# Up projections of two squared-ReLU feed-forwards: eight block products against seven

## What is computed

```
h    = rms_norm(x, g)                      # x: 512 tokens x 1024
u    = relu(h @ w1)                        # w1: 1024 x 4096
x    = x + (u * u) @ w2                    # w2: 4096 x 1024
```

## Time and profile before

| | |
|---|---|
| three runs | 2274.29, 2274.32, 2277.49 us; median 2274.32 |
| profiled execution: span from first to last instruction | 2272.1 us |
| its own time around the span | not given apart; the median of the runs is 2.2 us over the span |
| TensorE busy | 2247.1 us, 99% |
| VectorE / ScalarE / GpSimd busy | 1230.8 / 777.3 / 168.5 us |
| granted TensorE clock | tenths of 9 (90% and more) in all 40 slices |

### The profile page before, as it was taken

How to read it: one execution, slowest core, us unless ns; L and a number is a source line. 1 busy time by engine, 2 the same in 40 slices (tenths; PEclk the granted TensorE clock), 3 DMA queues, 4 the chain that set the end, 5 groups by cost and what they waited for, 6 DMA issues and landing times.

```text
span 2272.1 us, 28489 instructions
## 1 busy us (share of the span) xinstructions
PE 2247.1 (99%) x11659; PEld 1825.8 (80%) x11659; DVE 1230.8 (54%) x1464; ACT 777.3 (34%) x1024; POOL 168.5 (7%) x135
## 2 busy tenths in 40 slices
PE   9999999999999999999999999999999999999999
PEld 7888888878888888887876788888877868888888
DVE  6434446597543355575567644344468864544443
ACT  4222234244422323353247322222334573212221
POOL 2000001030100100020011100000101201000000
PEclk9999999999999999999999999999999999999999
DMA  5223223310323232232320232232233102323322
GB/s 188 93 93 106 97 79 99 93 61 20 102 92 105 82 109 93 75 110 93 104 65 20 78 107 93 93 100 87 87 106 89 61 20 65 102 93 95 108 86 81
DMA packets 193332, 200.56 MB, mean 88 GB/s; under 512 B 6370, under 2 KB 187378, under 8 KB 193236
## 3 DMA queue, kind: packets, MB, share of 16 engines
q1 hardware_dynamic: 193236, 199.22, 27.7%
HBM read 191.93 MB, written 2.10 MB: 85 GB/s over the span
## 4 chain that ended last, share of the span: by engine, by line
PE 93%; DVE 5%; ACT 1%; issue 1%; DMA 0%; SPq 0%; DVEq 0%; ACTq 0%
PE psum L684 92%; DVE sm L2477 1%; DVE rstd L1976 0%; DVE w_lo L296 0%; PE psum L1165 0%; PE psum L1173 0%; DVE free_x L1958 0%; ACT free_h L1449 0%; DVE free_h L1961 0%; DVE free_x L2599 0%; DVE sm L2597 0%; DVE sm L2303 0%; PE psum L916 0%; DVE xg_lo L1958 0%; DMA gains<-in_gains 0%
## 5 line engine op out<-in xcount | busy, mean ns | idle before, releaser
L684 PE MATMUL psum<-xg_lo,w_hi 128*128 128x512 f32 (+1 forms) x1576 | 608.4, 389 | 0.4 <-ACT free_x L1449 0.4
L684 PE MATMUL psum<-xg_hi,w_hi 128*128 128x512 f32 (+1 forms) x1528 | 596.0, 390 | 4.3 <-DVE xg_lo L1958 1.7
L684 PE MATMUL psum<-xg_hi,w_lo 128*128 128x512 f32 (+1 forms) x1528 | 592.9, 388 | 0.0
L288 ACT ACTIVATE w_hi<-w_raw 128x2048 fp32r<-128x2048 f32 (+1 forms) x178 | 338.7, 1903 | 478.0 <-PE psum L684 478.0
L296 DVE TENSOR_TENSOR w_lo<-w_raw,w_hi 128x2048 fp32r<-128x2048 f32 (+1 forms) x176 | 403.5, 2293 | 162.2 <-ACT w_hi L288 159.0
L684 PE MATMUL psum<-h_hi,w_hi 128*128 128x512 f32 x1144 | 451.7, 395 | 0.3 <-DVE h_lo L1958 0.3
L684 PE MATMUL psum<-h_hi,w_lo 128*128 128x512 f32 x1144 | 445.6, 389 | 0.0
L684 PE MATMUL psum<-h_lo,w_hi 128*128 128x512 f32 x1144 | 445.6, 389 | 0.0
L684 PEld LDWEIGHTS psum<-xg_lo,w_hi 128*128 128x128 f32 x1576 | 295.6, 188 | 62.2 <-ACT free_x L1449 1.4
L684 PEld LDWEIGHTS psum<-xg_hi,w_hi 128*128 128x128 f32 x1528 | 286.9, 188 | 68.9 <-issue 4.6
L684 PEld LDWEIGHTS psum<-xg_hi,w_lo 128*128 128x128 f32 x1528 | 286.9, 188 | 59.1
(11 more groups left out here) (309 smaller groups left out, 2106.8 us busy)
## 6 DMA issues: line engine op xcount, KB each, us to landing
w_raw<-in_mlp_w SPq DMA_DIRECT2D x64, 1024.0 KB, 5.4
w_raw<-in_ffn_w_gate SPq DMA_DIRECT2D x21, 1024.0 KB, 5.3
w_raw<-in_ffn_w_up SPq DMA_DIRECT2D x21, 1024.0 KB, 5.3
w_raw<-in_ffn_w_down SPq DMA_DIRECT2D x16, 1024.0 KB, 5.2
w_raw<-in_diff_w_in SPq DMA_DIRECT2D x12, 1024.0 KB, 5.1
w_raw<-in_w_in SPq DMA_DIRECT2D x9, 1024.0 KB, 5.2
w_raw<-in_dsa_w_in SPq DMA_DIRECT2D x9, 1024.0 KB, 5.1
w_raw<-in_ffn_w_down SPq DMA_DIRECT2D x8, 768.0 KB, 4.5
```

The costliest lines, as they stand in the source:

```text
L288: e.activation(w_hi[:, c % 2, 0:n], w_raw[:, c % 2, 0:n], ACT.Copy).then_inc(sem("hi_done"), 1)
L684: return pe.matmul(out, lhsT, rhs, start=start, stop=stop)
```

## The change

In both feed-forwards, two up blocks at a time (512 hidden features) are computed as a 2x2 block product with seven products in place of eight. The contraction tiles are halved by parity (even and odd k), the 512 tokens in two halves of 256, the hidden features in the two blocks. A product is then 4 k by 2 m by 3 = 24 matmuls of 256 columns.

- **Weights.** A block's load becomes two quarter loads of 512 KB (`fast_loads`). Seven operands a pair ("strips" of 1024 elements a partition) are split high and low: three are raw quarters, four are sums of quarters made by GpSimd (`w_sums`) in the arena. `w_hi` and `w_lo` are used as four strip slots, each free again when its product is done.
- **x.** In `wout2` and `wout3` ScalarE writes the scaled tiles to a buffer, VectorE makes three sums for each pair of tiles (four instructions of 256 columns), then come the split of the plain tiles (1024 elements) and of the sums (768 elements): `fin_sums`, `x_sums`.
- **Results.** ScalarE copies four intermediate results a pair out of PSUM, VectorE adds two of them to other banks, GpSimd adds two. VectorE then applies max(.,0) and `rstd`, and ScalarE squares and makes the high part.
- **Order.** GpSimd's weight sums of the first pair stand between its sums of squares. The loops of these feed-forwards are written out. Several semaphores elsewhere are merged (the constants' loads, the gate, the seed steps); what waits on them waits on the sum.

The core of the diff:

```diff
+        def strip_lo(e, c0, n):
...
+            e.tensor_tensor(lo_, strip_source(pair, i)[0], hi_.bitcast(F32),
+                            ALU.subtract).then_inc(strip_mark("lo", pair, i)[0], 1)
...
+            def fin_sums(p, i):
+                for m in range(2):
+                    a(x_raw(i)[:, m, :], x_res[:, 2 * i + m, :], ACT.Copy,
+                      scale=ngain(p, 2 * i + m)).then_inc(sem("x_scaled"), 1)
+                for t in (2 * i, 2 * i + 1):
...
+                    a(sq[:, t % 2, :], x_res[:, t, :], ACT.Square).then_inc(sem("sq_done"), 1)
+                act.wait_ge(sem("x_sums"), 4 * n + 2)
+                a(xg(p)[0][:, 2 * i:2 * i + 2, :], x_raw(i)[:], ACT.Copy).then_inc(sem("xg_hi_done"), 1)
+                act.wait_ge(sem("x_sums"), 4 * n + 4)
+                a(sx_hi[:, :, i, :], x_sum(i), ACT.Copy).then_inc(sem("xg_hi_done"), 1)
...
+            def x_sums(p, i):
+                tt(z[:, 0, :], e2, o2, ALU.add).then_inc(sem("x_sums"), 1)
+                tt(e2, e1, e2, ALU.subtract).then_inc(sem("x_sums"), 1)
+                dve.wait_ge(sem("x_sums"), 4 * n + 1)
+                tt(z[:, 1, :], z[:, 0, :], e1, ALU.subtract).then_inc(sem("x_sums"), 1)
+                dve.wait_ge(sem("x_sums"), 4 * n + 3)
+                tt(z[:, 2, :], o1, z[:, 1, :], ALU.subtract).then_inc(sem("x_sums"), 1)
...
@@ residual (VectorE)
+                if p_next in FAST.values():
+                    x_sums(p_next, i)
+                    if i < 3 and not split_first:
+                        lo(dve, c + 2 + i)
+                    fin_sums(p_next, i)
+                    if i == 3:
+                        lo(dve, c + 2 + i)
+                    return
...
@@ TensorE, one pair
+                    product(0, range(4))
+                    product(1, range(4))
+                    pe.wait_ge(sem("p_copied"), 4 * pair + 1)
+                    product(2, range(4))
...
+                    pe.wait_ge(sem("p_copied"), 4 * pair + 4)
+                    product(6, range(4))
...
@@ ScalarE, one pair
+                    if q:
+                        split(7 * q + 3)
+                        square(q - 1, 1)
+                    copy(pair, 0, chain, buf_c[:, 0, :])
+                    split(7 * q + 4)
+                    copy(pair, 1, second, buf_c[:, 1, :])
+                    split(7 * q + 5)
+                    copy(pair, 2, chain, buf_d[:, 0, :])
...
+                    split(7 * q + 6)
+                    split(7 * q + 7)
+                    copy(pair, 3, chain, buf_d[:, 1, :])
+                    if q == len(made) - 1:
+                        hi(act, after)
+                    split(7 * q + 8)
+                    split(7 * q + 9)
+                    square(q, 0)
...
@@ GpSimd
+                    if t == 3:
+                        w_sums(pair, (0, 1))
+                    if t == 5:
+                        w_sums(pair, (2, 3))
...
+                        if q + 1 < len(made):
+                            w_sums(pair + 1, (0, 1, 2))
+                        pool.wait_ge(sem("p_copied"), 4 * pair + 4)
...
+                        pool.tensor_tensor(buf_a[:, :, TS:S], by_halves(buf_d[:, 1, :]), by_halves(buf_c[:, 1, :]),
+                                           ALU.add).then_inc(sem("half_p"), 1)
+                        if q + 1 < len(made):
+                            w_sums(pair + 1, (3,))
+                    if g + 1 < len(GROUPS2):
+                        w_sums(made[-1] + 1, range(4))
```

More of the change, by code:

```diff
@@ L125, in gain_columns @@
     return np.ascontiguousarray(g.T)
+FAST = {"mlp0": 5, "mlp1": 7}
 def plan():
@@ new lines, in pairs_of, with wside, raw, strip @@
+        def pairs_of(c0):
+            first = fast_groups[c0]
+            return [i for i in range(first, len(pair_block)) if pair_block[i] - c0 in (2 * (i - first),)
+                    and (i == first or pair_block[i] not in fast_groups)]
+        def wside(c):
+            return (c + turned[c]) % 2
+        def raw(c, half):
+            return w_raw[:, c % 2, half * Q:(half + 1) * Q]
+        def strip(c0, n):
+            s_ = (2 * wside(c0) + n) % 4
+            cols = slice((s_ % 2) * Q, (s_ % 2 + 1) * Q)
+            return w_hi[:, s_ // 2, cols], w_lo[:, s_ // 2, cols]
@@ L283, in hi @@
                 return
+            for c0 in (c, c - 1):
+                if isinstance(j, int) and c0 in fast_groups:
+                    for n in range(2):
+                        strip_hi(e, c0, 2 * (c - c0) + n)
+                    return
             e.wait_ge(sem(f"landed{c % 2}"), 16 * j + 16 * (c // 2 + 1))
@@ L536, in ffn @@
                     else:
[L537 to L540, removed]
+                        fast_loads(c, rows(wu, 0, KT)[:, :, P * f0:P * (f0 + tiles)])
                     c = at[name, g, "down"]
@@ L764, in ffn @@
                     waits = {0: [(sem("h_done"), h0 + tiles // 2 - 1)], tiles - 2: [(sem("h_done"), h0 + tiles // 2)]}
+                    if name in FAST:
+                        waits = {k: [(sem("h_done"), h0 + max(2, k // 2 + 1))] for k in (0, 4, 6)}
                     c = at[name, g, "down"]
@@ new lines, in fast_up, with split, copy, square @@
+            def fast_up(c0, p, entry, h0):
+                made = pairs_of(c0)
+                after = c0 + 2 * len(made)
+                def split(n):
+                    if n < 7 * len(made):
+                        strip_hi(act, c0, n)
+                def copy(pair, j, src, dst):
+                    act.wait_ge(*strip_mark("pe", pair, (0, 1, 2, 4)[j]))
+                    if pair:
+                        act.wait_ge(*((sem("half_c"), pair) if j == 0 else (sem("half_p"), pair) if j in (1, 3) else
+                                      (sem("evac"), pair_block[pair - 1] + 1)))
+                    a(dst, src, ACT.Copy).then_inc(sem("p_copied"), 1)
+                def square(q, s_):
+                    v, n = (buf_a, buf_b)[s_], h0 + 2 * q + s_
+                    act.wait_ge(sem("hmul"), n + 1)
+                    a(v[:], v[:], ACT.Square).then_inc(sem("h_sq"), 1)
+                    act.wait_ge(sem("h_sq"), 2 * (fast_groups[c0] + q) + s_ + 1)
+                    a(hidden(p)[0][:, 4 * q + 2 * s_:4 * q + 2 * s_ + 2, :], v[:], ACT.Copy).then_inc(sem("h_hi_done"), 1)
+                for q, pair in enumerate(made):
+                    chain, second, third = pair_banks(c0, q)
+                    if q:
[6 more added lines that the diff above has]
+                    copy(pair, 2, chain, buf_d[:, 0, :])
+                    if entry and q == 0:
+                        stats(p)
+                    split(7 * q + 6)
[6 more added lines that the diff above has]
+                    square(q, 0)
+                square(len(made) - 1, 1)
+                hi(act, after + 1)
@@ L2730, in _, with add_squares @@
         def _(pool):
-            def add_squares(ready, done, r0, d0, dst):
+            def add_squares(ready, done, r0, d0, dst, between=None):
                 for t in range(1, KT):
@@ L2831, in _ @@
             sua_rounded()
-            fin(5)
+            fast_fin(5)
+            fast_up("mlp0")
             fin(6)
```

372 lines of the change are left out of this document (299 added, 73 removed).

## The result

The changed kernel takes 2311.39 us (median of 4 runs, 2308.94 to 2311.99) where the kernel before takes 2275.18 beside it (4 runs): ratio 1.0154, 95% interval 1.014 to 1.0169. It is slower by 36 us. The profiled execution is the one of 2311.99 us; its span is 2310.2 us.

What follows compares the result with a forecast made beforehand. It took TensorE's number and pitch of matmuls as the bound. Terms -25.6 + 17.7 + 20.6 + 14.8 + 4.2 = +31.7 on a span of 2272.1 gave 2303.8, so a median of 2306 us, range 2255 to 2320.

Steps and rivals of the forecast that it cites:

- Part 1: TensorE's up blocks: 168 matmuls of 256 columns replace 96 of 512, gaining 1.60 us a pair, -25.6 us for 16 pairs.
- The -38: Alternative estimate of the matmul gain in the up blocks, from isolated-matmul times of 109 and 216 ns: some 38 us.
- Part 2: VectorE and GpSimd, both reading two SBUF operands, take turns; GpSimd holds 2.27 us and VectorE 1.08 for 1024 elements.
- Rival A: Entries and groups: GpSimd's turns don't fall on the path, so the kernel is faster, 2258.8 us; chance 0.24.
- Part 3: Feed-forward entries: TensorE waits for the longer VectorE and ScalarE chain plus GpSimd's turns, 17.7 us in `mlp1`, 20.6 in `mlp0`.
- part 5: Clock after the last long wait of each entry: matmuls run at a lower level, +4.2 us in all, bounds 0 and 12.
- Part 4: Groups: TensorE waits before product 2 for ScalarE's copy of product 0, 1.5 us a group, 14.8 for both feed-forwards.
- Rival C: Groups: the down block's low part is late after a further GpSimd turn in each of 8, 2332 us; chance 0.08.
- Squares on ScalarE: Groups: moving the squares from VectorE to ScalarE was claimed to save VectorE nothing on the path.

Runs made afterwards that it cites:

- experiment 11: Changed kernel with first groups at eight products, copy of product 0 first, VectorE making second pairs' weight sums, whole computation done: 2256.43 us, 0.9909 of the kernel before.
- Experiment 1: Changed kernel with GpSimd writing one column of each weight sum in place of 1024, and a 2048-column fill before each entry: 2269.91 us, 0.9969 of the kernel before.
- Experiment 7: Changed kernel with unread 512-column matmuls put where TensorE would wait, at both entries and before product 2 of each second pair: 2307.58 us, 1.0142 of the kernel before.
- experiment 3: Changed kernel with ScalarE copying product 0 before strip 3 and the previous pair's square in each second pair: 2296.98 us, 1.0095 of the kernel before.
- experiment 8: Changed kernel with VectorE making the squares in place of ScalarE: 2336.87 us, 1.027 of the kernel before.
- experiment 6: Changed kernel with GpSimd copying the first operand of each weight sum in place of subtracting the second from it: 2277.90 us, 1.0015 of the kernel before.

## Why the prediction was right

Forecast 2306, measured 2311.4, on the side and by the mechanism forecast. That the number is so near is partly luck: several terms are off by 3 to 8 us and partly offset each other. Step by step:

- **Part 1, -25.6.** Right in kind, a little small. Without waits two pairs take 39.99 us [experiment 11], pitch 0.119, which makes -28.2 for 16 pairs. The -38 by the Trainium skill, "TensorE: Matmul & The Clock Gate", section "Back-to-back issue gap", was further off, as the rows had said. The seven starts a pair cost nothing.
- **Part 2, the turns.** Right: VectorE's instructions end 1.1 us after GpSimd's, and GpSimd's 3.39 us at 1414.40 end 2.27 after VectorE's split (1413.22 + 2.31). Experiment 1 prices them: 41.5 us come back. Rival A (turns off the path) fell with it, and its 2258.8 was too low even without the sums: 2269.9, because the entries alone keep 16 us of waits and slow spells of 7, where I had 10.1.
- **Part 3, the entries, 38.3.** Measured 31.4 of waits, 7 less than forecast, and 11.0 of slow spells, 7 more than part 5 had. Together 42.4 against 38.3 + 4.2 = 42.5: the sum is right because the two errors cancel, which is luck. Experiment 7 suggests that the chain of VectorE sets the whole of it, since the entries lose as much with fewer slow spells; then this part is 4 too small and part 5's term does not lie here. The longest wait was forecast at 7.5 and is 7.2 in `mlp0` and 5.8 in `mlp1`, for tiles 6 and 7, ended by VectorE as said; block 3, the first strip and tiles 4 and 5 were waited for too, as said. The quarter loads landed after 4.5 us (4.9 in the first entry), not 3.6, which the text had priced at 3 us; no run tests whether they are what is missing. The written sum is also 0.2 too high (54.0 - 37.0 + 0.5 is 17.5, not 17.7).
- **Part 4, a group, 14.8.** The place and the chain are right (ScalarE's copy behind square and high part, experiment 3). The size is not: 1.8 to 2.3 us in place of 1.5 (2.6 in the first), 17.9 in all, and the slow spells behind three of these waits, which the step had at nothing, 5.2. Both together are 8 us over the step. **This is the term that was mis-sized**; the 2.6 us by which part 1 was too small offset a third of it. The chain had one square and one high part ahead of the copy, 4.0 us from VectorE's lateness on. In the trace ScalarE has two of each and a strip, and from the end of VectorE's `buf_a` (1418.88) to the end of the copy (1424.53) it is 5.6 us. VectorE's own lateness was put too high in return: `buf_a` ends 2.2 us after product 6 (its last matmul is at 1416.38 + 0.28), not 3.1. So the copy is done 7.9 us after product 6 in place of 7.2.
- **Part 5, the clock, +4.2 net.** Experiment 7 gives 3.8 us for what it took away of the low clock, about the forecast, but by luck: the seat is wrong. I had it behind the last long wait of each entry. Behind those it hides in VectorE's lateness, and it is paid in the groups, after waits of 2.0 to 2.3 us, to which I had given no low clock. The last of the earlier trace rows could have told me: there the granted clock is 0.53 from 2.3 us after TensorE's last matmul on.
- **Rival C** (2332) had the right neighbour: experiment 8 adds work to VectorE in a first pair, and the groups' waits grow, a down block becomes late, and the time is 2337.
- **Squares on ScalarE "save VectorE nothing on the path"** was wrong: they save 25.5 us against VectorE squaring within this scheme. The sentence compared with the kernel before, where VectorE had room.

What stays open: why a slow spell follows some waits of 2.0 to 2.3 us and not others (three of eight in the kernel after, all eight with waits of 3.0 to 3.8), and what the slow spells that experiment 7 left at the entries cost.

## What to carry to other kernels

When work is taken from the bounding engine and given to the others, lay out the others' lists in order at the places where they have least room, here the entry, where VectorE already had 8 of 10.9 us to do: apply the change where there is room and leave the tight place as it was. With the first group left as it was, the copy put first and half of the weight sums moved to VectorE, +36 us became -19; the copy is worth 14 of these 55 (experiment 3) and the sums some 2, so most comes from the first group. On an engine that works in order, put the short step that the bounding engine waits for ahead of the long ones it does not. And count work on GpSimd that reads SBUF as time taken from VectorE, by its hold, wherever VectorE reads two operands from SBUF at the same time.

## What was not expected of the hardware

- After a wait of TensorE of 2.33 us the granted clock went down, and late: in the third group TensorE restarts at 1510.74 at 0.12 a matmul and goes over to 0.213 at 1512.0, until 1515.4 (granted clock 0.51 over 1512.0 to 1515.4, the level of 1.2 GHz). After one of 2.30 us, in the group before, it did not.

```profile
1510.74 0.36 PE L906 MATMUL psum<-sx_hi,w_hi 128*128 128x256 f32 x1 [2.33 <-ACT buf_c L1649]
...
1511.87 0.34 PE L906 MATMUL psum<-sx_hi,w_hi 128*128 128x256 f32 x1
1512.00 0.42 PE L907 MATMUL psum<-sx_lo,w_hi 128*128 128x256 f32 x1
```

- GpSimd's copy of 1024 elements holds VectorE for 0.9 us, its subtraction of two operands for 2.27 (experiment 6), and its clearing of 2048, which reads nothing, not at all (experiment 1): the kind of operation sets the price.
- A load of 512 KB took 4.5 us to land where one of 1024 KB took 5.1: half the bytes saved 0.6 us.
